# Two of the five feed-forwards: three matmuls of 288, 256 and 272 columns in place of three of 272, with the first 16 tokens' share added by VectorE

## The chip, the core and the metric

One core of one Trainium2 chip runs the whole program: TensorE (PE, with its weight loads shown apart as PEld), VectorE (DVE), ScalarE (ACT), GpSimd (POOL) and SyncE (SP, which issues the loads of the weights). The metric is the device time of one execution in microseconds; the median of the runs shown counts.

## What is computed

The reference runs two blocks after one another on one sequence of 256 tokens, 1024 wide. The first block puts 16 learned tokens (`meta`) ahead of the sequence and drops them at its end, so its layers work on 272 tokens, except the last feed-forward, of which only 256 tokens are needed.

```
h = concat(meta, x)                                    # 16 + 256 tokens
for l in range(2):
    h = h + 0.5 * swiglu(rmsnorm(h), ffn1_gate, ffn1_up, ffn1_down)
    h = h + hybrid_mixer(rmsnorm(h), ...)
    h = h + 0.5 * swiglu(rmsnorm(h), ffn2_gate, ffn2_up, ffn2_down)
x = rmsnorm(h)[:, 16:]
# then second_block(x): ffn, attention, ffn, ffn, retention, ffn, on 256 tokens
swiglu(x) = (silu(x @ w_gate) * (x @ w_up)) @ w_down   # 1024 -> 2816 -> 1024
```

## The kernel before

The program is a list of phases (`PHASES`), numbered y: 0 feed-forward, 1 mixer, 2 feed-forward, 3 feed-forward, 4 mixer, 5 feed-forward, and so on. Tokens lie along the columns, so a phase with all tokens has matmuls of 272 columns (y = 0 to 4) and the later ones 256 (`first_col`, `width`). The change is about y = 2 and y = 3.

Each float32 operand is split in two parts, a high one and the rest, the low one: the weights into `whi` and `wlo` (ACT copies `raw` to `whi`, L435, and DVE subtracts, L442), the input into `u` (ACT L467, DVE L480) and the hidden values into `hid` (ACT L1187, DVE L1669). A product of one 128 by 128 weight tile then takes three matmuls that add up in one PSUM bank, here called a triple: high weights with the high input (L419), high weights with the low input (L426), low weights with the high input (L427). `products` writes them, and each brings its own weight load.

A feed-forward streams its weights in panels through a ring of four (`RING`). A gate or up panel has 8 weight tiles, a down panel 11. The 44 gate and up panels come first (`gate_up`): for each pair, called a tile here, DVE multiplies both results by the norm's factor `R` (`gt` L1658, `up` L1660), ACT takes the Silu (`sl` L1182), DVE multiplies (`pr` L1665), and both split the product into `hid`. Between these DVE and ACT split the panels four ahead. Then 16 down panels give 8 tiles of the output (`out_proj`), which DVE adds to `h` (L1625); ACT and DVE split the new `h` at once into the next phase's `u`, and POOL sums its squares (L521, L524) for the next norm, which PE averages with a matmul (L562) behind the next phase's first panel. A feed-forward has 44 × 8 + 16 × 11 = 528 triples.

The order on each engine is the order in which the code is written; semaphores tie the engines together. PE waits for a split panel (`lo_ready`), for an emptied bank (`a_evac`: the one used four panels before) and, in a phase's first panel, for `u_ready`: for six of the eight tiles of `u` at its first weight tile, and for the last two at weight tiles 6 and 7. `U_PLACE` and `HID_PLACE` say at how many columns past the start of the buffer the high part stands, and by how many more the low part is shifted; tiles lie 320 columns apart in phases 0 to 4.

## Time and profile before

| | |
|---|---|
| median of 3 runs | 2170.9 us (2170.79 to 2171.69) |
| the profiled execution's own time | 2170.45 us |
| its span, first to last instruction | 2168.7 us |
| PE busy | 2157.2 us, 99% of the span, 18129 matmuls |
| DVE, ACT, POOL busy | 1471.9, 1205.7, 283.8 us |
| matmuls of 272 columns in `u` and `hid` | 1504 and 528 of each line of the triple |

Busy time of PE counts a matmul from its start to the end of its last column, and neighbours overlap, so a row's mean of 281 ns is no pace. The pace of a run of matmuls is read from their start times: the time from one start to the next, or a stretch divided by the number of starts in it. The profiled execution is 0.45 us below the median and lies 1.75 us above its own span.

### The profile page before, as it was taken

What the parts mean: (1) busy time and instruction counts of PE and PEld (TensorE: products, weight loads), DVE (VectorE), ACT (ScalarE), POOL (GpSimd) and SP (SyncE); (2) the same over time, 40 slices, a digit from 0 to 9 for tenths busy, and PEclk for the clock granted to TensorE, in tenths of its full rate; (3) what the DMA queues carried; (4) which work ended last, traced back from release to release, by engine and by line L of the source; (5) the groups of instructions that cost most, each with busy time, mean ns of one, the idle gap of its engine ahead of it and who ended that gap; (6) DMA issues with size and microseconds to landing.
All of it is one profiled execution on the core that took longest, in us unless ns stands there. A gap on an engine that the chain in (4) does not pass through costs nothing.

```text
span 2168.7 us, 48303 instructions
## 1 busy us (share of the span) xinstructions
PE 2157.2 (99%) x18129; PEld 2139.8 (99%) x18129; DVE 1471.9 (68%) x2242; ACT 1205.7 (56%) x1757; POOL 283.8 (13%) x328
## 2 busy tenths in 40 slices
PE   8999999999999999999999999999999999999999
PEld 8999999999999999999999999999999999999999
DVE  6655998665566579876657657976656745686663
ACT  6444786544444368855545547865455535465552
POOL 0001661100100136220020011010010010101000
PEclk9999999999999999999999999999999999999999
DMA  6555435555455554456656655356656655446563
GB/s 233 176 192 167 163 117 175 175 174 198 153 179 187 182 164 142 150 179 193 204 176 195 204 190 170 119 183 194 207 173 196 210 177 181 159 156 196 193 219 129
DMA packets 100401, 386.57 MB, mean 178 GB/s; under 512 B 11312, under 2 KB 12464, under 8 KB 100304
## 3 DMA queue, kind: packets, MB, share of 16 engines
q1 hardware_dynamic: 99648, 383.89, 54.0%
q0 software_dynamic: 368, 1.26, 0.2%
q8 instruction: 62, 1.02, 0.2%
q14 instruction: 35, 0.29, 0.0%
q10 hardware_dynamic: 288, 0.12, 0.0%
HBM read 384.18 MB, written 1.05 MB: 178 GB/s over the span
## 4 chain that ended last, share of the span: by engine, by line
PE 91%; DVE 6%; ACT 2%; issue 1%; DMA 0%; ACTq 0%; DVEq 0%
PE bank L426 28%; PE bank L427 28%; PE bank L419 28%; DVE wlo L442 2%; DVE bank L1723 1%; PE bank L1064 1%; PE bank L1066 1%; PE bank L1065 1%; ACT whi L435 1%; PE bank L1111 0%; PE bank L773 0%; DVE proj L1709 0%; PE bank L955 0%; PE bank L957 0%; PE bank L958 0%
## 5 line engine op out<-in xcount | busy, mean ns | idle before, releaser
L419 PE MATMUL bank<-u,whi 128*128 128x256 f32 (+2 forms) x3776 | 1062.6, 281 | 7.1 <-DVE u L480 7.1
L426 PE MATMUL bank<-u,whi 128*128 128x256 f32 (+1 forms) x3776 | 1062.0, 281 | 0.0
L427 PE MATMUL bank<-u,wlo 128*128 128x256 f32 (+1 forms) x3776 | 1060.0, 281 | 0.0
L442 DVE TENSOR_TENSOR wlo<-raw,whi 128x1024 fp32r<-128x1024 f32 (+1 forms) x677 | 891.7, 1319 | 187.2 <-ACT whi L435 186.6
L435 ACT ACTIVATE whi<-raw 128x1024 fp32r<-128x1024 f32 (+1 forms) x677 | 743.5, 1112 | 189.6 <-PE bank L427 168.8
L419 PEld LDWEIGHTS bank<-u,whi 128*128 128x128 f32 x3776 | 711.2, 188 | 8.5 <-DVE wlo L442 7.1
L426 PEld LDWEIGHTS bank<-u,whi 128*128 128x128 f32 x3776 | 711.1, 188 | 0.9 <-issue 0.2
L427 PEld LDWEIGHTS bank<-u,wlo 128*128 128x128 f32 x3776 | 710.9, 188 | 0.0
L419 PE MATMUL bank<-hid,whi 128*128 128x256 f32 (+1 forms) x1408 | 394.2, 280 | 0.0
L426 PE MATMUL bank<-hid,whi 128*128 128x256 f32 (+1 forms) x1408 | 394.2, 280 | 0.0
L427 PE MATMUL bank<-hid,wlo 128*128 128x256 f32 (+1 forms) x1408 | 394.2, 280 | 0.0
L1660 DVE TENSOR_TENSOR up<-bank,R 128x256 f32<-128x256 f32 (+1 forms) x176 | 75.7, 430 | 289.9 <-PE bank L427 289.9
L427 PEld LDWEIGHTS bank<-hid,wlo 128*128 128x128 f32 x1408 | 264.6, 188 | 0.0
L426 PEld LDWEIGHTS bank<-hid,whi 128*128 128x128 f32 x1408 | 264.6, 188 | 0.0
L419 PEld LDWEIGHTS bank<-hid,whi 128*128 128x128 f32 x1408 | 264.6, 188 | 0.0
L467 ACT ACTIVATE u<-h,gain 128x256 fp32r<-128x256 f32 (+1 forms) x88 | 44.2, 512 | 268.4 <-DVE h L1625 262.5
L1182 ACT ACTIVATE sl<-gt 128x256 f32<-128x256 f32 (+1 forms) x160 | 67.7, 423 | 197.8 <-DVE gt L1658 197.7
L1187 ACT ACTIVATE hid<-pr 128x256 f32 (+2 forms) x160 | 67.9, 424 | 152.8 <-DVE pr L1665 152.8
L1625 DVE SCALAR_TENSOR_TENSOR h<-bank,h 128x256 f32<-128x256 f32 (+1 forms) x88 | 37.8, 430 | 164.0 <-PE bank L427 163.9
L516 POOL TENSOR_TENSOR ssq<-h 128x256 f32<-128x256 f32 (+1 forms) x10 | 6.2, 624 | 1028.7 <-DVE h L1625 1028.7
L2170 POOL TENSOR_TENSOR proj<-proj,tprod 128x272 f32<-128x272 f32 (+1 forms) x120 | 121.4, 1032 | 54.9 <-ACT tprod L1225 50.0
L521 POOL TENSOR_TENSOR sq<-h 128x256 f32<-128x256 f32 (+1 forms) x70 | 45.1, 645 | 345.7 <-DVE h L1625 344.7
(298 smaller groups left out, 2187.7 us busy)
## 6 DMA issues: line engine op xcount, KB each, us to landing
raw<-w SPq DMA_DIRECT2D x552, 512.0 KB, 3.4
raw<-w SPq DMA_DIRECT2D x128, 704.0 KB, 4.7
h<-xT SPq DMA_DIRECT2D x4, 272.0 KB, 5.8
outT<-h SPq DMA_DIRECT2D x8, 128.0 KB, 4.7
consts<-cst POOLq DMA_DIRECT2D x1, 576.0 KB, 4.5
dist<-cst POOLq DMA_DIRECT2D x1, 192.0 KB, 2.8
rdist<-cst POOLq DMA_DIRECT2D x1, 192.0 KB, 4.1
sgain<-small POOLq DMA_DIRECT2D x1, 145.5 KB, 5.1
```

The lines of the kernel that those rows point to most:

```text
L419: pe.matmul(out[:, cut:cols], w, x[:, cut:cols], start=first, stop=False, skip_group_check=True)
L426: pe.matmul(out, w_h, x_lo, start=False, stop=False, skip_group_check=True)
L427: return pe.matmul(out, w_l, x_hi, start=False, stop=last, skip_group_check=True)
L435: act.activation(weights(0, n), raw[:, n % RING, 0:COLS[n]].rearrange("p (k c) -> p k c", c=128), ACT.Copy).then_inc(hi_ready, 1)
L442: dve.tensor_tensor(weights(1, n), raw[:, n % RING, 0:COLS[n]].rearrange("p (k c) -> p k c", c=128), weights(0, n), ALU.subtract).then_inc ...
L467: act.activation(u_at(y, 0, f), h[:, f, win(y)], ACT.Copy, scale=norm_gain(y, f)).then_inc(u_hi_ready, 1)
L521: pool.tensor_tensor(sq[:, win(y)], h[:, f, win(y)], h[:, f, win(y)], ALU.mult).then_inc(sq_done, 1)
L1182: act.activation(sl[:, p, W], gt[:, p, W], ACT.Silu).then_inc(silu_done, 1)
L1187: act.activation(hid_at(y, 0, f), pr[:, p, W], ACT.Copy).then_inc(hid_hi_ready, 1)
L1625: dve.scalar_tensor_tensor(out=h[:, f, W], in0=src, scalar=factor, in1=h[:, f, W], op0=ALU.mult, op1=ALU.add).then_inc(h_done, 1)
L1660: dve.tensor_tensor(up[:, p, W], bank[(g + 1) % 4][:, 0:N], R[:, W], ALU.mult).then_inc(a_evac, 1)
L2170: pool.tensor_tensor(acc, acc, tprod[:, m % TAP_RING, W2], ALU.add)\
```

## The change

In phases 2 and 3 (`JOINED`) the triple is made by `joined_products`. The low part of the first 16 tokens' input is no longer beside the other low values but in the 16 columns just ahead of the high part. One matmul with the high weights takes these 16 columns and the 272 high ones as one run of 288 columns; another takes the other 256 low columns; the low weights still meet 272 columns. The columns are 816 before and after. The bank then holds 16 columns more: the first tokens' low product in columns 0 to 15, and everything else in 16 to 287. DVE adds these 16 columns where it empties the bank, in an instruction of its own, and writes the low parts in two pieces. Phase 2 issues the 288 columns first, phase 3 the 256.

```diff
-U_PLACE = {0: (48, 0), 1: (48, 0), 2: (48, 0), 3: (48, 0), 4: (48, 0), 5: (48, 0), 6: (48, 0), 8: (48, 0), 9: (48, 0), 10: (48, 0), 11: (48, 0), 12: (48, 0), 7: (48, 0)}
+U_PLACE = {0: (48, 0), 1: (48, 0), 2: (48, -16), 3: (64, -32), 4: (48, 0), 5: (48, 0), 6: (48, 0), 8: (48, 0), 9: (48, 0), 10: (48, 0), 11: (48, 0), 12: (48, 0), 7: (48, 0)}
-HID_PLACE = {0: (24, 0), 2: (24, 0), 3: (24, 0), 5: (24, 0), 7: (24, 0), 9: (24, 0), 10: (24, 0), 12: (24, 0)}
+HID_PLACE = {0: (24, 0), 2: (24, -16), 3: (40, -32), 5: (24, 0), 7: (24, 0), 9: (24, 0), 10: (24, 0), 12: (24, 0)}
+JOINED = (2, 3)
+LONG_FIRST = {2: True, 3: False}
...
+        def joined_products(pe, out, n, k, x_hi, x_lo, first, last, long_first):
+            w_h, w_l = weights(0, n)[:, k, :], weights(1, n)[:, k, :]
+            long, short = (out[:, 0:META + T], with_ahead(x_hi)), (out[:, 2 * META:META + T], x_lo[:, META:T])
+            for i, (o, x) in enumerate((long, short) if long_first else (short, long)):
+                pe.matmul(o, w_h, x, start=(first and i == 0), stop=False, skip_group_check=True)
+            return pe.matmul(out[:, META:META + T], w_l, x_hi, start=False, stop=last, skip_group_check=True)
...
     def dve_update(dve, y, f):
+            if y in JOINED:
+                dve.scalar_tensor_tensor(out=ahead(u_at(y, 0, f)), in0=h[:, f, 0:META], scalar=norm_gain(y, f),
+                                         in1=u_at(y, 0, f, 0, META), op0=ALU.mult, op1=ALU.subtract)
+                dve.scalar_tensor_tensor(out=u_at(y, 1, f, META), in0=h[:, f, META:T], scalar=norm_gain(y, f),
+                                         in1=u_at(y, 0, f, META), op0=ALU.mult, op1=ALU.subtract).then_inc(u_ready, 1)
+                return
...
     def act_norm(act, y):
+            if y in JOINED:
+                act.activation(R_long[:, 0:META], NORM[:, 0:META], ACT.Ln, bias=rms_eps)
+                act.activation(R, NORM[:, 0:T], ACT.Ln, bias=rms_eps).then_inc(log_done, 1)
+                act.wait_ge(log_done, n)
+                act.activation(R_long[:, :], R_long[:, :], ACT.Exp, scale=-0.5).then_inc(R_ready, 1)
+                return
...
             def out_proj(y, n0, per_tile, factor, N, sources=None, done=None, split_ahead=0):
+                    if y in JOINED:
+                        src = bank[4 + f % 2]
+                        dve.scalar_tensor_tensor(out=h[:, f, 0:META], in0=src[:, 0:META], scalar=factor,
+                                                 in1=h[:, f, 0:META], op0=ALU.mult, op1=ALU.add).then_inc(first_added, 1)
+                        dve.scalar_tensor_tensor(out=h[:, f, META:T], in0=src[:, 2 * META:META + T], scalar=factor,
+                                                 in1=h[:, f, META:T], op0=ALU.mult, op1=ALU.add)
+                        dve.wait_ge(first_added, adds(y) + 2 * FT + f + 1)
+                        dve.scalar_tensor_tensor(out=h[:, f, 0:META], in0=src[:, META:2 * META], scalar=factor,
+                                                 in1=h[:, f, 0:META], op0=ALU.mult, op1=ALU.add).then_inc(h_done, 1)
...
                 def tile(n, g, F, f, p, it, last, split=True):
+                        if y in JOINED:
+                            dve.tensor_tensor(long[:, p, :], src[:, 0:META + T], R_long[:, :], ALU.mult).then_inc(a_evac, 1)
+                            dve.wait_ge(a_evac, g + i + 1 + it4)
+                            dve.tensor_tensor(out[:, p, 0:META], out[:, p, 0:META], long[:, p, 0:META], ALU.add)\
+                               .then_inc(first_added, 1)
...
+                    if y in JOINED:
+                        dve.tensor_tensor(ahead(hid_at(y, 0, f)), pr[:, p, 0:META], hid_at(y, 0, f)[:, 0:META], ALU.subtract)
+                        dve.tensor_tensor(hid_at(y, 1, f)[:, META:T], pr[:, p, META:T], hid_at(y, 0, f)[:, META:T],
+                                          ALU.subtract).then_inc(hid_ready, 1)
```

ACT's Silu and DVE's product wait for the adds (`first_added`) in place of `a_evac`. `R`, `gt` and `up` become parts of longer buffers `R_long`, `gt_long` and `up_long`, in all phases.

On PE the first two triples of phase 2 stand as follows before the change (rows name the operation, the bank it writes, the input and the weights it reads, and its output's size).

```order
L419 MATMUL bank<-u,whi 128x272
L426 MATMUL bank<-u,whi 128x272
L427 MATMUL bank<-u,wlo 128x272
L419 MATMUL bank<-u,whi 128x272
L426 MATMUL bank<-u,whi 128x272
L427 MATMUL bank<-u,wlo 128x272
```

After the change the same place reads so.

```order
L451 MATMUL bank<-u,whi 128x288
L451 MATMUL bank<-u,whi 128x256
L452 MATMUL bank<-u,wlo 128x272
L451 MATMUL bank<-u,whi 128x288
L451 MATMUL bank<-u,whi 128x256
L452 MATMUL bank<-u,wlo 128x272
```

Nothing moved from its place; only two of the three sizes are others. On DVE one tile of gate and up (the last but one of phase 2, where no loop counters stand between) is before the change:

```order
L1658 TENSOR_TENSOR gt<-bank,R 128x272
L1660 TENSOR_TENSOR up<-bank,R 128x272
L442 TENSOR_TENSOR wlo<-raw,whi 128x1408
L1665 TENSOR_TENSOR pr<-sl,up 128x272
L442 TENSOR_TENSOR wlo<-raw,whi 128x1408
L1669 TENSOR_TENSOR hid<-pr,hid 128x272
```

After it, the same tile:

```order
L1727 TENSOR_TENSOR gt_long<-bank,R_long 128x288
L1729 TENSOR_TENSOR gt_long<-gt_long 128x16
L1727 TENSOR_TENSOR up_long<-bank,R_long 128x288
L1729 TENSOR_TENSOR up_long<-up_long 128x16
L467 TENSOR_TENSOR wlo<-raw,whi 128x1408
L1740 TENSOR_TENSOR pr<-sl,up_long 128x272
L467 TENSOR_TENSOR wlo<-raw,whi 128x1408
L1745 TENSOR_TENSOR hid<-pr,hid 128x16
L1746 TENSOR_TENSOR hid<-pr,hid 128x256
```

Three instructions of 16 columns came in per tile, and both splits of panels stand behind two of them. On DVE the end of phase 2 (the last two tiles of `h`, the splits of phase 3's first panels and the last of its `u`) is before the change:

```order
L1625 SCALAR_TENSOR_TENSOR h<-bank,h 128x272
L442 TENSOR_TENSOR wlo<-raw,whi 128x1024
L480 SCALAR_TENSOR_TENSOR u<-h,gain,u 128x272
L442 TENSOR_TENSOR wlo<-raw,whi 128x1024
L1625 SCALAR_TENSOR_TENSOR h<-bank,h 128x272
L480 SCALAR_TENSOR_TENSOR u<-h,gain,u 128x272
L442 TENSOR_TENSOR wlo<-raw,whi 128x1024 x2
```

After it, from the last tile of `h` on:

```order
L1682 SCALAR_TENSOR_TENSOR h<-bank,h 128x16
L1684 SCALAR_TENSOR_TENSOR h<-bank,h 128x256
L1687 SCALAR_TENSOR_TENSOR h<-bank,h 128x16
L509 SCALAR_TENSOR_TENSOR u<-h,gain,u 128x16
L511 SCALAR_TENSOR_TENSOR u<-h,gain,u 128x256
L467 TENSOR_TENSOR wlo<-raw,whi 128x1024 x2
```

One instruction on `h` became three, and one on `u` became two; their order against the splits stays.

## Rows read from the trace of the kernel before

**Rows 1.** The page: busy time of each engine, TensorE's granted clock by slice.

```profile
PE 2157.2 (99%) x18129; PEld 2139.8 (99%) x18129; DVE 1471.9 (68%) x2242; ACT 1205.7 (56%) x1757; POOL 283.8 (13%) x328
PEclk9999999999999999999999999999999999999999
```

**Rows 2.** Timeline of PE: first matmul of phases 2, 3 and 4 (start, length).

```profile
384.98 0.29 PE L419 MATMUL bank<-u,whi 128*128 128x272 f32 x1
...
580.81 0.29 PE L419 MATMUL bank<-u,whi 128*128 128x272 f32 x1
...
776.63 0.29 PE L419 MATMUL bank<-u,whi 128*128 128x272 f32 x1
```

**Rows 3.** Busy time by stretch: phase 2 (272 columns) and 7 (256).

```profile
400.00:500.00 100.00, 100.00 (x813) 100.00 (x812) 63.34 (x103) 48.41 (x67) 0.00 (x0) 1.00 0.54 178
...
1220.00:1290.00 70.00, 70.00 (x620) 70.00 (x619) 42.98 (x57) 31.49 (x39) 4.75 (x8) 1.00 0.62 204
```

**Rows 4.** Timeline of PE: first and last of 43 matmuls of 512 columns.

```profile
1801.24 0.39 PE L1064 MATMUL bank<-whi,u 128*128 128x512 f32 x1
...
1810.86 0.39 PE L1064 MATMUL bank<-whi,u 128*128 128x512 f32 x1
```

**Rows 5.** Timeline of PEld: weight loads behind two matmuls of 288 columns, and the next.

```profile
259.63 0.19 PEld L419 LDWEIGHTS bank<-u,whi 128*128 128x128 f32 x1
...
259.76 0.19 PEld L426 LDWEIGHTS bank<-u,whi 128*128 128x128 f32 x1
...
879.19 0.19 PEld L419 LDWEIGHTS bank<-u,whi 128*128 128x128 f32 x1
...
879.33 0.19 PEld L426 LDWEIGHTS bank<-u,whi 128*128 128x128 f32 x1
```

**Rows 6.** Timeline of PE, phases 1 and 4: first and last of 10, 11, 10.

```profile
284.64 0.29 PE L427 MATMUL bank<-u,wlo 128*128 128x272 f32 x1
...
285.78 0.29 PE L427 MATMUL bank<-u,wlo 128*128 128x272 f32 x1
...
897.01 0.28 PE L427 MATMUL bank<-u,wlo 128*128 128x256 f32 x1
...
898.19 0.28 PE L419 MATMUL bank<-u,whi 128*128 128x256 f32 x1
...
903.90 0.28 PE L427 MATMUL bank<-u,wlo 128*128 128x256 f32 x1
...
904.92 0.28 PE L427 MATMUL bank<-u,wlo 128*128 128x256 f32 x1
```

**Rows 7.** Timeline of DVE in phase 2: one tile, and the idle time before.

```profile
450.77 0.44 DVE L1660 TENSOR_TENSOR up<-bank,R 128x272 f32<-128x272 f32 x1 [2.16 <-PE bank L427]
...
456.69 0.44 DVE L1660 TENSOR_TENSOR up<-bank,R 128x272 f32<-128x272 f32 x1 [2.15 <-PE bank L427]
```

**Rows 8.** DVE's instructions by form: busy, mean ns of one.

```profile
L1665 DVE TENSOR_TENSOR pr<-sl,up 128x256 f32<-128x256 f32 x110 | 46.0, 418 | 0.0
...
L1665 DVE TENSOR_TENSOR pr<-sl,up 128x272 f32<-128x272 f32 x66 | 28.7, 434 | 0.7 <-ACT sl L1182 0.7
...
L1931 DVE TENSOR_SCALAR dst<-dst,lam 128x2 f32<-128x2 f32 x8 | 1.8, 229 | 0.3
```

**Rows 9.** Timeline from phase 2 to 3, by engine.

```profile
581.01 0.44 DVE L1625 SCALAR_TENSOR_TENSOR h<-bank,h 128x272 f32<-128x272 f32 x1 [3.38 <-PE bank L427]
582.04 0.50 DVE L480 SCALAR_TENSOR_TENSOR u<-h,gain,u 128x272 fp32r<-128x272 f32 x1 [0.59 <-ACT u L467]
...
582.25 0.93 POOL L524 TENSOR_TENSOR ssq<-ssq,sq 128x272 f32<-128x272 f32 x1
...
583.40 0.28 PE L419 MATMUL bank<-u,whi 128*128 128x272 f32 x1
...
583.77 0.39 PE L562 MATMUL bank<-ssq,consts 128*128 128x272 f32 x1
```

More of the change, by code:

```diff
@@ L396, in hid_at, with ahead, with_ahead @@
             return tile_of(hid, FT, TILE_STEP if y <= LAST_MIX else SEQ, HID_PLACE[y], y, part, f, first_col(y), T)
+        def ahead(whole):
+            return bass.AP(whole.tensor, whole.offset - META, [whole.ap[0], [1, META]])
+        def with_ahead(whole):
+            return bass.AP(whole.tensor, whole.offset - META, [whole.ap[0], [1, META + T]])
         def width(y):
@@ L451, in da_square, with adds @@
             return dqk[:, f // 2, f % 2, :] if f < 4 else (dsq if f < 6 else drq)[:, f % 2, :]
+        def adds(y):
+            return (2 * FT + KD) * JOINED.index(y)
         def norm_gain(y, f):
@@ L683, in tile @@
                                 pe.wait_ge(ready, count - (lag if K == 0 else last - K))
+                            if y in JOINED:
+                                mm = joined_products(pe, bank[4 + j % 2], n, k, x(0, K), x(1, K),
+                                                     K == 0, K == last, LONG_FIRST[y])
+                                continue
                             mm = products(pe, bank[4 + j % 2][:, 0:N], n, k, x(0, K), x(1, K),
@@ L1198, in ffn @@
                     n = b["P"] + 2 * f
-                    act.wait_ge(a_evac, b["A"] + 2 * f + 1)
+                    if y in JOINED:
+                        act.wait_ge(first_added, adds(y) + 2 * f + 1)
+                    else:
+                        act.wait_ge(a_evac, b["A"] + 2 * f + 1)
                     act.activation(sl[:, p, W], gt[:, p, W], ACT.Silu).then_inc(silu_done, 1)
@@ L1624, in out_proj @@
                     dve.wait_ge(panel_used, n0 + (done[f] if done else per_tile * (f + 1)))
-                    dve.scalar_tensor_tensor(out=h[:, f, W], in0=src, scalar=factor,
-                                             in1=h[:, f, W], op0=ALU.mult, op1=ALU.add).then_inc(h_done, 1)
+                    if y in JOINED:
+                        src = bank[4 + f % 2]
[6 more added lines that the diff above has]
+                                                 in1=h[:, f, 0:META], op0=ALU.mult, op1=ALU.add).then_inc(h_done, 1)
+                    else:
+                        dve.scalar_tensor_tensor(out=h[:, f, W], in0=src, scalar=factor,
+                                                 in1=h[:, f, W], op0=ALU.mult, op1=ALU.add).then_inc(h_done, 1)
                     if per_tile == 1 and f > 0:
@@ L1656, in tile @@
                     it4, it2 = (RING * it, 2 * it) if not last else (0, 0)
-                    dve.wait_ge(panel_used, n + 1 + it4)
-                    dve.tensor_tensor(gt[:, p, W], bank[g % 4][:, 0:N], R[:, W], ALU.mult).then_inc(a_evac, 1)
-                    dve.wait_ge(panel_used, n + 2 + it4)
-                    dve.tensor_tensor(up[:, p, W], bank[(g + 1) % 4][:, 0:N], R[:, W], ALU.mult).then_inc(a_evac, 1)
+                    for i, (out, long) in enumerate(((gt, gt_long), (up, up_long))):
+                        src = bank[(g + i) % 4]
+                        dve.wait_ge(panel_used, n + i + 1 + it4)
+                        if y in JOINED:
+                            dve.tensor_tensor(long[:, p, :], src[:, 0:META + T], R_long[:, :], ALU.mult).then_inc(a_evac, 1)
+                            dve.wait_ge(a_evac, g + i + 1 + it4)
+                            dve.tensor_tensor(out[:, p, 0:META], out[:, p, 0:META], long[:, p, 0:META], ALU.add)\
+                               .then_inc(first_added, 1)
+                        else:
+                            dve.tensor_tensor(out[:, p, W], src[:, 0:N], R[:, W], ALU.mult).then_inc(a_evac, 1)
                     if split:
@@ L1663, in tile @@
                     dve.wait_ge(silu_done, F + 1 + it2)
-                    dve.wait_ge(a_evac, g + 2 + it4)
+                    if y in JOINED:
+                        dve.wait_ge(first_added, adds(y) + 2 * (f if last else p) + 2 + it4)
+                    else:
+                        dve.wait_ge(a_evac, g + 2 + it4)
                     dve.tensor_tensor(pr[:, p, W], sl[:, p, W], up[:, p, W], ALU.mult).then_inc(prod_done, 1)
```

23 lines of the change are left out of this document (17 added, 6 removed).

## The prediction

> **What bounds the kernel now.** I read the page first: PE is busy for 99% of the span, at the upper level of its granted clock (2.4 GHz) in every slice [rows 1]. So the question is what a triple costs, and whether anything makes PE wait. The timeline of PE at the ends of phases 2 and 3 gives the place of the change: phase 2 runs from 384.98 to 580.81 us, phase 3 from there to 776.63 us, 195.8 us each [rows 2]. The list of waits for that stretch is empty on PE: inside the two phases PE waits for nobody, and a faster engine elsewhere would be worth nothing. Only shorter matmuls help.
>
> The busy time by stretch gives their pace. In a stretch of 100 us of phase 2, 813 matmuls lie wholly or in part. A matmul is shown for about 0.29 us, so 2.3 of them are open at any moment, and 100 / (813 − 2.3) gives 123.3 ns from start to start. For 256 columns it is 70 / (620 − 2.4) = 113.3 ns [rows 3]. 512 columns take 42 starts in 9.62 us, 229.0 ns each [rows 4]. So 512 columns cost twice 256 and 1% more, while the 16 columns from 256 to 272 cost 10.0 ns, where a sixteenth of 113.3 would be 7.1. That is the odd size: 272 pays about 2.9 ns that 256 does not.
>
> **The change on PE.** A phase has 528 triples, two phases 1056. Before, a triple costs 3 × 123.3 = 370.0 ns. Now it has 288, 256 and 272 columns. Two sizes have rows: 113.3 and 123.3. For 288 there is no stream in the trace, so I bound it:
> - by the line from 256 to 512 columns, 113.3 + 32 × (229.0 − 113.3) / 256 = 127.8 ns, that is 9 times a 32nd column at a pace of 256's;
> - by the line from 272 to 512, 123.3 + 16 × (229.0 − 123.3) / 240 = 130.3 ns, if 288 carries 272's surcharge along;
> - by a second step of 10.0 ns, 133.3 ns.
>
> There are a few single matmuls of 288 columns (L730, in the mixers). The weight load behind one and the one after it lie 0.13 us apart in one place and 0.14 in another [rows 5], which bounds it by 125 and 145 and decides little, but does not point above the third. I take 127.8, since 256 and 512, both whole multiples of 32 columns, lie on one line and 288 is such a multiple too. The triple is then 127.8 + 113.3 + 123.3 = 364.4 ns, 5.6 ns less, and 1056 × 5.6 = 5.9 us less. By the second bound the triple is 366.9 and the gain 3.3 us; by the third it is 369.9 and the gain nothing.
>
> The Trainium skill speaks against this change: "TensorE: Matmul & The Clock Gate", section "Back-to-back issue gap", gives N / 2.4 + 2.5 ns for an isolated warm matmul of N columns. By it 272 columns would take 115.8 ns and the sum depends on the columns alone, 816 before and after, so that PE would gain nothing. This trace disagrees with both its size (123.3) and its slope (10.0 ns for 16 columns after 256).
>
> **VectorE.** Per tile of gate and up it gets three instructions of 16 columns and two that grow by 16. The growth is 434 − 418 = 16 ns each. The nearest small instruction, on 2 columns, takes 229 ns; the 16 columns by their slope alone would take 16 ns [rows 8]. I take 200 ns each, with the wait of each add for its own engine's result in it: 0.6 + 0.03 us per tile, between 0.1 and 0.9. The cover is DVE's idle time before it empties the up panel, 2.16 us in each tile's 5.92 us [rows 7]; behind the waiting instruction stand the split of the panel four ahead and ACT's Silu, which PE needs two panels later. About 1.5 us of cover remain, 1.3 in the worst case. So this costs nothing; without the cover it would be 44 × 0.63 = 28 us.
>
> **The two ends.** When a phase ends, the last tile of `h` is updated (581.01 us), ACT and DVE split it (DVE's part starts at 582.04 and ends at 582.54), and PE needs it at 583.40, weight tile 7 of the next first panel. POOL's last sum ends at 583.18, and PE's norm matmul starts at 583.77 [rows 9]. The update becomes three instructions, which adds about 0.38 us (0.05 to 0.46), and the split of `u` in two adds 0.2 more into phase 3. Then `u` is ready at 583.1 and the sum at 583.6: both in time, by 0.3 and 0.2 us. If the small instructions are slower than I think, PE stalls by some tenths twice; I put 0.1 us for both. ACT's extra logarithm of 16 columns delays the first emptied bank by less than 0.5 us, and PE comes back to that bank four panels, 11.8 us, after the phase's start. The 8 further small instructions on `u` at the end of phase 1 come one per panel of 24 matmuls, 3.0 us; with 0.2 us each I count nothing for them. No DMA is added; SP's loads wait for the splits as before.
>
> **The sum.** The profiled execution's 2170.45 us − 5.9 + 0.1 = 2164.65 us; the median of the runs is 0.45 above the profiled one, so 2165.1 us.
>
> **The rivals.**
> - *288 costs more than the line* (130 to 132 ns). For it: 272 does not lie on the line either, and where the place of the columns against the weights changes from triple to triple, as it now does within a triple (288 starts 16 columns ahead of the others in phase 2, 272 starts 16 behind in phase 3), some surcharge may come back. Gain 1.5 to 3.3 us: 2168 to 2169.5 us.
> - *Only the sum of the columns counts.* Then 288 costs a second 10.0 ns and the triple 369.9: 2171 us, and the change does nothing, which is also what the skill's formula says. Against it: 512 columns would have to cost 113.3 + 16 × 10.0 = 273 ns, and they cost 229.0.
> - *PE falls into its slower pace.* The trace shows that the same matmul has two paces at the same granted clock. In the mixers 272 columns ran at 1.14 / 9 = 126.7 ns for a whole panel, and 256 columns at 1.18 / 10 = 118.0 ns, while the same line 6 us later has 1.02 / 9 = 113.3 [rows 6]. Each pace holds until something interrupts the stream. In phases 2 and 3 all 272-column matmuls ran at the faster pace; the change shifts starts by 16 columns against the weights, and the norm matmul behind the first panel interrupts once per phase. Locked in the slower pace from there, a triple costs about 132 (127.8 and the 4.7 of the 256) + 118.0 + 126.7 = 377, 7 ns more than before, and both phases 7.4 us more: 2178 us. One phase of the two: near 2172. The change loses from 44% of the triples on (5.6 against 7.0).
> - *VectorE or the ends make PE wait.* 0.5 us at each end at most, or a tile's worth if the cover were gone; 2166 to 2172 us.
>
> **How the numbers follow.** The line (2164 to 2166.5 us) gets 0.43; the dearer 288, 0.24; columns alone, 0.14; the slower pace in one phase 0.06, in both 0.08; waits 0.05. Runs of this kernel agree within 0.04%, and about 0.2%, 4.3 us, is what a measurement can tell from no change. Faster by more than that is below 2166.6: the line and a little of the second and of the waits, 0.48. Slower is above 2175.2: 0.09. The rest, 0.43, is within. My range is 2162.5 to 2171.8: below, 272 may lose its surcharge too when its neighbours are whole multiples (2.9 ns × 1056 = 3.1 us, half of which I allow); above, it ends past the cases of columns alone and one slow phase. Left out are about 0.08 above and 0.05 below and at the edges of waits. The likeliest case's own range is 2164 to 2166.5.
>
> **What the changed profile would show.** Right: phases 2 and 3 last 192.8 us each in place of 195.8; in a stretch of 100 us of either, about 825 matmuls in place of 813; the 256 columns at 113.3 ns; DVE's idle time before `up` still above 1 us per tile; no wait of PE inside the phases. The step that fails first if I am wrong is the price of 288: from 133 ns on there is no gain. A pace of 118 for the 256 columns would show the slower pace, by phase, since the two phases differ in order and places; a gap on PE at either end longer than that around the norm matmul now would show the ends.

## The result and the profile after

The changed kernel takes 2179.1 us (median of 7 runs, 2178.01 to 2179.78), the kernel before 2171.1 us in the same comparison (7 runs, 2170.68 to 2172.55). The ratio is 1.0035 with a 95% interval of 1.0026 to 1.0044: slower by 8.0 us, where 2165.1 was forecast and the range ended at 2171.8. The profiled execution took 2179.65 us, its span is 2177.9.

The page, for [rows 1]: PE is still busy for 99%, at the upper level of its clock throughout. Its busy time grew by 8.0 us with the same number of matmuls. DVE has 180 instructions more.

```profile
PE 2165.2 (99%) x18129; PEld 2147.5 (99%) x18129; DVE 1504.1 (69%) x2422; ACT 1206.6 (55%) x1759; POOL 278.9 (13%) x328
...
PEclk9999999999999999999999999999999999999999
```

Busy time by stretch of the changed kernel, in the columns of [rows 3]: phase 2, phase 3, phase 7.

```profile
400.00:500.00 100.00, 100.00 (x813) 100.00 (x813) 72.27 (x153) 48.44 (x68) 0.00 (x0) 1.00 0.55 178
600.00:700.00 100.00, 100.00 (x792) 100.00 (x791) 69.78 (x149) 47.99 (x67) 0.00 (x0) 1.00 0.55 175
...
1220.00:1290.00 70.00, 70.00 (x620) 70.00 (x619) 43.13 (x61) 33.17 (x41) 3.33 (x5) 1.00 0.64 207
```

Phase 2 has the 813 starts that it had before, where 825 were forecast; by the prediction's own formula that is again 123.3 ns a matmul, 370.0 a triple. Phase 3 fell to 792, 100 / (792 − 2.3) = 126.6 ns, 380 a triple. Phase 7 is untouched.

The timeline of PE shows the sizes one by one (a row with x2 holds two matmuls of one line, its start is that of the first): phase 2, long one first, and phase 3, short one first.

```profile
451.15 0.28 PE L451 MATMUL bank<-u,whi 128*128 128x256 f32 x1
451.26 0.28 PE L452 MATMUL bank<-u,wlo 128*128 128x272 f32 x1
451.38 0.41 PE L451 MATMUL bank<-u,whi 128*128 128x288 f32 x2
451.63 0.29 PE L452 MATMUL bank<-u,wlo 128*128 128x272 f32 x1
...
782.79 0.29 PE L451 MATMUL bank<-hid,whi 128*128 128x288 f32 x1
782.92 0.29 PE L452 MATMUL bank<-hid,wlo 128*128 128x272 f32 x1
783.05 0.42 PE L451 MATMUL bank<-hid,whi 128*128 128x256 f32 x2
783.30 0.29 PE L452 MATMUL bank<-hid,wlo 128*128 128x272 f32 x1
```

The 256 columns start at 451.15, the 272 behind them at 451.26, the next 288 at 451.38, and one 272 to the next is 0.37 us. In phase 3 that is 0.38. The start times of a whole stretch, which the trace has in ns, give the means: in phase 2 288 columns take 133.0 ns, 256 take 114.5, 272 take 122.5, together 370.0; in phase 3 130.0, 123 and 127, together 380.

The list of waits from 383 to 800 us was empty on PE before. Now it has one row, and the timeline shows where: the start of phase 2, in its first panel.

```profile
PE bank L451 <- DVE u L511: 1.5, 3, 0.6
```
```profile
384.84 0.29 PE L444 MATMUL bank<-qk,wlo 128*128 128x272 f32 x1
385.74 0.49 PE L451 MATMUL bank<-u,whi 128*128 128x288 f32 x2 [0.61 <-DVE u L511]
...
387.91 0.28 PE L452 MATMUL bank<-u,wlo 128*128 128x272 f32 x1
388.70 0.52 PE L451 MATMUL bank<-u,whi 128*128 128x288 f32 x2 [0.51 <-DVE u L511]
389.06 0.28 PE L452 MATMUL bank<-u,wlo 128*128 128x272 f32 x1
389.76 0.52 PE L451 MATMUL bank<-u,whi 128*128 128x288 f32 x2 [0.42 <-DVE u L511]
...
390.24 0.39 PE L596 MATMUL bank<-ssq,consts 128*128 128x272 f32 x1
...
787.16 0.39 PE L596 MATMUL bank<-ssq,consts 128*128 128x272 f32 x1
```

PE's starts are 0.90, 0.79 and 0.70 us apart at the three gaps, and the first matmul behind each takes some 0.1 us longer. DVE's last `u` part had come too late, and the timeline of DVE says why. First the changed kernel, then the kernel before, each from one split of a weight panel to the next:

```profile
379.38 1.80 DVE L467 TENSOR_TENSOR wlo<-raw,whi 128x1024 fp32r<-128x1024 f32 x1
381.10 0.43 DVE L1690 SCALAR_TENSOR_TENSOR h<-bank,h 128x272 f32<-128x272 f32 x1
381.45 0.22 DVE L509 SCALAR_TENSOR_TENSOR u<-h,gain,u 128x16 fp32r<-128x16 f32 x1
381.59 0.93 DVE L511 SCALAR_TENSOR_TENSOR u<-h,gain,u 128x256 fp32r<-128x256 f32 x1
382.45 1.79 DVE L467 TENSOR_TENSOR wlo<-raw,whi 128x1024 fp32r<-128x1024 f32 x1
```
```profile
380.37 1.28 DVE L442 TENSOR_TENSOR wlo<-raw,whi 128x1024 fp32r<-128x1024 f32 x1 [0.30 <-ACT whi L435]
382.20 0.44 DVE L1625 SCALAR_TENSOR_TENSOR h<-bank,h 128x272 f32<-128x272 f32 x1 [0.55 <-PE bank L427]
382.55 0.49 DVE L480 SCALAR_TENSOR_TENSOR u<-h,gain,u 128x272 fp32r<-128x272 f32 x1
383.35 1.28 DVE L442 TENSOR_TENSOR wlo<-raw,whi 128x1024 fp32r<-128x1024 f32 x1 [0.30 <-ACT whi L435]
```

Before, DVE waited twice in the panel shown, of 2.98 us, 0.30 for ACT and 0.55 for PE: PE set the pace. Now there is no wait left in its 3.07 us; DVE is the slower one. The small instruction itself takes only 0.14 us from start to start. But the split went from 1.28 to 1.79 and the `u` part from 0.49 to 0.93, with fewer columns. POOL, which squares and adds `h` at the same time, went the other way: its square (L521 before, L555 now) took 0.83 us and takes 0.64, its sum (L524, L558) took 1.63 and takes 0.84. First the kernel before, then the changed one:

```profile
379.73 0.83 POOL L521 TENSOR_TENSOR sq<-h 128x272 f32<-128x272 f32 x1 [0.29 <-DVE h L1625]
380.64 1.63 POOL L524 TENSOR_TENSOR ssq<-ssq,sq 128x272 f32<-128x272 f32 x1
```
```profile
379.25 0.84 POOL L558 TENSOR_TENSOR ssq<-ssq,sq 128x272 f32<-128x272 f32 x1
381.60 0.64 POOL L555 TENSOR_TENSOR sq<-h 128x272 f32<-128x272 f32 x1 [1.51 <-DVE h L1690]
```

**Where the 9.2 us between the two spans lie**, by the starts of the norm matmuls: from that of phase 1 to that of phase 2 181.87 us in place of 179.49 (+2.4, the stall); to that of phase 3 195.89 in place of 195.82 (+0.1); to that of phase 4 201.03 in place of 195.83 (+5.2); the other 1.5 in code that the change does not touch, of which 1.3 in one stretch near the end, between the norm matmuls that start at 1791.87 and 1988.32 us before: 196.45 us, now 197.77.

DVE inside phase 2, for [rows 7] and [rows 8]: one tile from its first emptied bank on.

```profile
450.83 0.46 DVE L1727 TENSOR_TENSOR gt_long<-bank,R_long 128x288 f32<-128x288 f32 x1
451.33 0.17 DVE L1729 TENSOR_TENSOR gt_long<-gt_long 128x16 f32<-128x16 f32 x1
453.06 0.46 DVE L1727 TENSOR_TENSOR up_long<-bank,R_long 128x288 f32<-128x288 f32 x1 [1.56 <-PE bank L452]
```

The idle time before `up` went from 2.16 to 1.56 us: the 0.6 us of the forecast, and still hidden. The end of phase 2, for [rows 9]:

```profile
583.30 0.17 DVE L1682 SCALAR_TENSOR_TENSOR h<-bank,h 128x16 f32<-128x16 f32 x1 [3.11 <-PE bank L452]
583.39 0.41 DVE L1684 SCALAR_TENSOR_TENSOR h<-bank,h 128x256 f32<-128x256 f32 x1
...
584.63 0.48 DVE L511 SCALAR_TENSOR_TENSOR u<-h,gain,u 128x256 fp32r<-128x256 f32 x1
584.69 1.05 POOL L558 TENSOR_TENSOR ssq<-ssq,sq 128x272 f32<-128x272 f32 x1
586.13 0.62 PE L596 MATMUL bank<-ssq,consts 128*128 128x272 f32 x2
```

Phase 3 starts at 583.10, so that its eighth triple is due 7 × 0.38 us later, at 585.76; `u` is ready at 585.11, the sum at 585.74, the norm matmul runs at 586.13. No gap.

### The profile page after: what moved, and what is told of

Same layout as the page of the kernel before. It is cut to its first block, busy times and chain, and to the rows that moved or that the text cites. A ratio compares the mean times of both kernels' runs of the same rounds, so it can differ in the third digit from the quotient of the medians.

```text
span 2177.9 us, 48605 instructions
## 1 busy us (share of the span) xinstructions
PE 2165.2 (99%) x18129; PEld 2147.5 (99%) x18129; DVE 1504.1 (69%) x2422; ACT 1206.6 (55%) x1759; POOL 278.9 (13%) x328
## 4 chain that ended last, share of the span: by engine, by line
PE 90%; DVE 7%; ACT 2%; issue 1%; DMA 0%; ACTq 0%; DVEq 0%
PE bank L443 22%; PE bank L444 22%; PE bank L436 22%; PE bank L451 12%; PE bank L452 6%; DVE wlo L467 3%; DVE bank L1803 1%; ACT whi L460 1%; PE bank L1113 1%; PE bank L1115 1%; PE bank L1114 1%; PE bank L1160 0%; PE bank L822 0%; DVE proj L1789 0%; PE bank L1004 0%
## 5 line engine op out<-in xcount | busy, mean ns | idle before, releaser
L436 PE MATMUL bank<-u,whi 128*128 128x256 f32 (+1 forms) x3072 | 860.4, 280 | 7.1 <-DVE u L514 7.1
L443 PE MATMUL bank<-u,whi 128*128 128x256 f32 (+1 forms) x3072 | 860.4, 280 | 0.0
L444 PE MATMUL bank<-u,wlo 128*128 128x256 f32 (+1 forms) x3072 | 858.3, 279 | 0.0
L444 PEld LDWEIGHTS bank<-u,wlo 128*128 128x128 f32 x3072 | 578.5, 188 | 0.0
L436 PE MATMUL bank<-hid,whi 128*128 128x256 f32 (+1 forms) x1056 | 293.3, 278 | 0.0
L443 PE MATMUL bank<-hid,whi 128*128 128x256 f32 (+1 forms) x1056 | 293.3, 278 | 0.0
L444 PE MATMUL bank<-hid,wlo 128*128 128x256 f32 (+1 forms) x1056 | 293.3, 278 | 0.0
L451 PE MATMUL bank<-u,whi 128*128 128x288 f32 (+1 forms) x1408 | 264.9, 287 | 1.5 <-DVE u L511 1.5
L452 PE MATMUL bank<-u,wlo 128*128 128x272 f32 x704 | 202.9, 288 | 0.0
L443 PEld LDWEIGHTS bank<-hid,whi 128*128 128x128 f32 x1056 | 198.3, 188 | 0.0
L444 PEld LDWEIGHTS bank<-hid,wlo 128*128 128x128 f32 x1056 | 198.3, 188 | 0.0
L436 PEld LDWEIGHTS bank<-hid,whi 128*128 128x128 f32 x1056 | 198.3, 188 | 0.0
L1234 ACT ACTIVATE sl<-gt_long 128x256 f32<-128x256 f32 (+1 forms) x160 | 67.7, 423 | 212.1 <-DVE gt_long L1732 149.5
```

The source lines that it names most:

```text
L436: pe.matmul(out[:, cut:cols], w, x[:, cut:cols], start=first, stop=False, skip_group_check=True)
L443: pe.matmul(out, w_h, x_lo, start=False, stop=False, skip_group_check=True)
L444: return pe.matmul(out, w_l, x_hi, start=False, stop=last, skip_group_check=True)
L451: pe.matmul(o, w_h, x, start=(first and i == 0), stop=False, skip_group_check=True)
L452: return pe.matmul(out[:, META:META + T], w_l, x_hi, start=False, stop=last, skip_group_check=True)
L1234: act.activation(sl[:, p, W], gt[:, p, W], ACT.Silu).then_inc(silu_done, 1)
```

## The experiments

My theory after this profile was that 288 columns cost more than the line by themselves; the rivals were the start columns of the streamed operand, which now differ within a triple, the order, and the columns of the bank. The first four kernels ask for these one by one. Each ran once, beside a run of the kernel before at 2170.12 us on the same chip.

**Whole sizes.** All three matmuls of a triple read the long piece in phase 2, two of three in phase 3.

```diff
+            if long_first:
+                pe.matmul(long[0], w_h, long[1], start=first, ...)
+                pe.matmul(long[0], w_h, long[1], start=False, ...)
+                return pe.matmul(long[0], w_l, long[1], ...)
...
-            return pe.matmul(out[:, META:META + T], w_l, x_hi, ...)
+            return pe.matmul(long[0], w_l, long[1], ...)
```

> This kernel leaves out part of the sums: in phase 2 all three matmuls of a triple are 288 columns from the same place into the same columns (the low product of 256 tokens is left out and the high one taken twice); in phase 3 the triple is 256, 288 and 288. Theory 'starts': sizes that are whole multiples of 32 cost what the line says (127.8 and 113.3 ns) as long as neighbours start at the same place; the surcharge in the changed kernel comes from starts that move by 16 columns from one matmul to the next. Then phase 2 has 128 ns per matmul (about 784 matmuls in 100 us) and phase 3 keeps a surcharge, since 256 and 288 start at one place and the last at another only by the place of the first column. Theory 'size': 288 columns cost 130 to 133 ns in any company: phase 2 at 131 to 133 (755 to 766 in 100 us). Theory 'half step': only the 272 columns, no multiple of 32, upset their neighbours: phase 3 at (113.3 + 127.8 + 127.8) / 3 = 123.0 (816 in 100 us). In both theories with a surcharge phase 3 is at 127 or more (790 or fewer).

2193.72 us. The stretch of phase 2:

```profile
400.00:500.00 100.00, 100.00 (x753) 100.00 (x752) 67.12 (x142) 44.45 (x63) 0.00 (x0) 1.00 0.51 163
```

753 starts are 133.2 ns for each 288, all from one start column and to one bank column. In phase 3 it took 131 and 132, the 256 beside it 117. So 288 is dear without unequal neighbours too: the line's 127.8 was wrong for this stream.

**Shift alone.** The kernel before, three times 272, with the low parts 16 columns off against the high ones (in phase 2 the high ones were moved, in phase 3 the low ones).

```diff
-U_PLACE   2: (48, 0),  3: (48, 0)      HID_PLACE   2: (24, 0), 3: (24, 0)
+U_PLACE   2: (32, 16), 3: (48, -16)    HID_PLACE   2: (8, 16), 3: (24, -16)
```

> The kernel before with three matmuls of 272 columns; only the low inputs of phase 2 start 16 columns later, and those of phase 3 16 columns earlier, against the high ones (modulo 64 columns). Theory 'starts': the pace gets worse without any change in size, from 123.3 ns to 125 to 127 in at least one of the phases (790 to 802 matmuls in 100 us). Theories 'size' and 'half step': nothing changes, 123.3 ns (813).

2175.79 us.

```profile
400.00:500.00 100.00, 100.00 (x799) 100.00 (x798) 61.54 (x100) 47.65 (x67) 0.00 (x0) 1.00 0.55 178
600.00:700.00 100.00, 100.00 (x805) 100.00 (x805) 62.44 (x101) 48.48 (x67) 0.00 (x0) 1.00 0.55 176
```

Without any new size a matmul went from 123.3 to 125.5 ns in phase 2 and to 124.4 in phase 3 (by the start times); single ones lie between 120 and 130. So the starts seem to have a part too. It is one execution; against it stand nine phases of the old triple, in seven profiles of this case, all at 123.3.

**Orders swapped**, and **bank columns alike**.

```diff
-LONG_FIRST = {2: True, 3: False}
+LONG_FIRST = {2: False, 3: True}
```

> The changed kernel with the 256 columns first in phase 2 and the 288 first in phase 3, the places unchanged. If the order alone made phase 3 slow (126.6 ns per matmul against 123.3 in phase 2), the two phases trade paces: 792 matmuls in 100 us of phase 2, 813 of phase 3. If the places made it ('starts'), phase 3 stays near 792 and phase 2 near 813. Theory 'size' says neither moves.

2182.29 us. Phase 2 now has 792 starts in 100 us (256 at 117.0, 288 at 136.0, 272 at 127.0: 380.0), phase 3 has 799 (376.7). The 380 went with the order, but phase 3 did not get phase 2's 370 for it.

```diff
-            long, short = (...), (out[:, 2 * META:META + T], x_lo[:, META:T])
+            long, short = (...), (out[:, 0:SEQ], x_lo[:, META:T])
...
-            return pe.matmul(out[:, META:META + T], w_l, x_hi, ...)
+            return pe.matmul(out[:, 0:T], w_l, x_hi, ...)
```

> The changed kernel with all three outputs of a triple starting at the bank's column 0 in place of 0, 32 and 16 (the columns are then added up wrongly; only the time counts). If the place in PSUM makes the surcharge, both phases get faster, towards 121.5 ns (825 in 100 us). By the theories 'starts', 'size' and 'half step' nothing changes: 813 and 792.

2180.47 us, 813 and 792 starts as in the changed kernel. The bank's columns play no part.

The next four shared a run of the kernel before at 2171.25 us.

**Phase 2 alone.**

```diff
-U_PLACE   3: (64, -32)    HID_PLACE   3: (40, -32)
-JOINED = (2, 3)
+U_PLACE   3: (48, 0)     HID_PLACE   3: (24, 0)
+JOINED = (2,)
```

> Only phase 2 joined; phase 3 is that of the kernel before. Theory 'two causes' (a stall of some 2.3 us at the end of phase 1, and phase 3's pace of 126.6 ns): the stall stays, phase 2 has 813 matmuls in its stretch of 100 us, phase 3 has 813 too, and the time is 2.3 to 2.7 us over the kernel before. Rival 'a pace carried along' (phase 3 is slow because of what phase 2 left PE in): phase 3 stays near 792 to 800 and the time is 5 us or more over before.

2173.41 us, 2.2 over; the same three gaps at the end of phase 1, 813 starts in both phases. Phase 2's stream costs nothing and gains nothing; the stall is the whole loss.

**Phase 3 alone, made like phase 2.**

```diff
-JOINED = (2, 3)
-LONG_FIRST = {2: True, 3: False}
-U_PLACE   2: (48, -16), 3: (64, -32)    HID_PLACE   2: (24, -16), 3: (40, -32)
+JOINED = (3,)
+LONG_FIRST = {3: True}
+U_PLACE   2: (48, 0),   3: (48, -16)    HID_PLACE   2: (24, 0),   3: (24, -16)
```

> Only phase 3 joined, with phase 2's places and the long one first; phase 2 is that of the kernel before. Theory 'two causes': no stall at the end of phase 1, since the small instructions on u now stand at the end of phase 2; phase 3 runs at 370 ns a triple, 813 in 100 us; the time is that of the kernel before within 0.7 us. Rival 'any joined phase costs a stall ahead of it': 2 us over before, with gaps on PE at the end of phase 2. Rival 'phase 3 itself is slower': about 792 in 100 us and 5 us over before.

2176.02 us, 4.8 over. No gap on PE, as expected, but 799 starts in phase 3: triples of 368 and 385 ns in turn, 376.7 on average, where the same instructions at the same places took 368 and 372 in phase 2. My theory of two fixed causes fell here: one stream has two paces.

**Other places** (long one first in both phases).

```diff
-U_PLACE   2: (48, -16), 3: (64, -32)    HID_PLACE   2: (24, -16), 3: (40, -32)
+U_PLACE   2: (16, -16), 3: (16, 16)     HID_PLACE   2: (72, -16), 3: (72, 0)
```

> Both phases joined, the long one first, with other start columns: counted modulo 64 from a boundary of 256 bytes, 288 starts at 32 and 256 and 272 at 48 (phase 2, gate and up), 288 at 48 and both others at 0 (phase 2, down), 288 at 32, 256 at 16, 272 at 48 (phase 3, gate and up), 288 at 48, 256 at 16, 272 at 0 (phase 3, down). Theory 'size and place': 288 keeps 130 to 134 ns wherever it starts, 256 and 272 are at 113 to 123 and 122 to 128, and no stretch gets below 368 ns a triple (817 in 100 us). Rival 'place alone': 288 falls to 128 in at least one of the four places, and that stretch runs at 365 ns a triple or less (825 or more in 100 us). The stall at the end of phase 1 stays in both.

2178.59 us. The triples took 373.4 (gate and up) and 377.8 (down) in phase 2, 373.3 and 380.0 in phase 3; the 288 averaged 132.5 to 135.9. None is under 370, and one comes to 380 with the long one first.

**Eight small instructions** in the kernel before.

```diff
+            if y == 2:
+                hi = u_at(y, 0, f, 0, META)
+                dve.scalar_tensor_tensor(out=bass.AP(hi.tensor, hi.offset - META, [hi.ap[0], [1, META]]), in0=h[:, f, 0:META],
+                                         scalar=norm_gain(y, f), in1=hi, ...)
```

> The kernel before with one thing more: at the end of phase 1 eight DVE instructions of 16 columns on u, one ahead of each of the eight instructions that make u's low part for phase 2; nobody reads what they write, and the place is the gap ahead of u. Theory 'the extra instruction makes DVE the bound there': a panel costs DVE 3.0 to 3.1 us where PE wants 2.96, PE stalls near 385 to 389 us, and the time is 1 to 2.5 us over before. Rival 'it is the shifted start and the shorter form of the big instruction, or the split weights, not the extra one': no gap on PE there, within 0.4 us of before.

2173.47 us, 2.2 over. The list of waits on PE from 383 to 800 us, and DVE's timeline:

```profile
PE bank L419 <- DVE u L485: 1.6, 3, 0.7
```
```profile
379.74 1.79 DVE L442 TENSOR_TENSOR wlo<-raw,whi 128x1024 fp32r<-128x1024 f32 x1
381.46 0.43 DVE L1630 SCALAR_TENSOR_TENSOR h<-bank,h 128x272 f32<-128x272 f32 x1
381.81 0.22 DVE L482 SCALAR_TENSOR_TENSOR u<-h,gain,u 128x16 fp32r<-128x16 f32 x1
381.95 0.95 DVE L485 SCALAR_TENSOR_TENSOR u<-h,gain,u 128x272 fp32r<-128x272 f32 x1
```

The same three gaps and the same 1.79 and 0.95 us: the extra instruction is enough for the stall, without the shifted parts or the shorter form.

It does not always bring it, though. Of the twelve profiles with such an instruction at the end of phase 1 eleven have the stall; the run with whole sizes, which changes nothing there, has not. Its list of waits on PE from 383 to 800 us is empty, and from phase 1's norm matmul to phase 2's it took 179.81 us, 0.3 more than before. In its first panel, and in the four behind it, POOL had the long times:

```profile
369.59 0.48 DVE L515 SCALAR_TENSOR_TENSOR u<-h,gain,u 128x256 fp32r<-128x256 f32 x1
...
369.61 0.96 POOL L559 TENSOR_TENSOR sq<-h 128x272 f32<-128x272 f32 x1 [1.65 <-DVE h L1694]
370.65 1.63 POOL L562 TENSOR_TENSOR ssq<-ssq,sq 128x272 f32<-128x272 f32 x1
```

DVE gained time in these panels and met the long times only from 382.96 us on, too late to hold up PE. So the same instructions have two outcomes.

The next four, beside 2172.57 us, asked for the two paces and for what a size costs.

**Both phases like phase 2** (long one first, phase 2's places in phase 3).

```diff
-LONG_FIRST = {2: True, 3: False}
-U_PLACE   3: (64, -32)    HID_PLACE   3: (40, -32)
+LONG_FIRST = {2: True, 3: True}
+U_PLACE   3: (48, -16)    HID_PLACE   3: (24, -16)
```

> Both phases joined with phase 2's places and the long matmul first, so that phase 3 goes on in the stream that phase 2 ends in. Theory 'the pace is set where the stream begins, and carried' (the run with only phase 3 joined had the same instructions at 376.3 ns a triple that phase 2 runs at 370.0): phase 3 keeps phase 2's 370 ns, 813 matmuls in its stretch of 100 us, and the time is that of the run with phase 2 alone joined, 2.2 us over before. Rival 'the pace belongs to phase 3 itself, its weights or banks': about 799 in 100 us and 5.3 us over before. The stall at the end of phase 1 stays in both.

2176.28 us, and neither theory had it:

```profile
400.00:500.00 100.00, 100.00 (x799) 100.00 (x798) 71.68 (x151) 47.57 (x67) 0.00 (x0) 1.00 0.55 173
600.00:700.00 100.00, 100.00 (x813) 100.00 (x813) 72.42 (x152) 49.02 (x70) 0.00 (x0) 1.00 0.56 181
```

This time phase 2 is the slow one and phase 3 the fast. The starts tell when it changed: phase 2 ran at 369 and 371 ns up to its first gaps, and at 368 and 385 from the norm matmul (390.4 us) on; phase 3 kept 368 and 385 up to its norm matmul (589.7 us) and ran at 368 and 372 behind it. An interruption can change the pace, in either direction.

**A pause ahead of phase 3**: PE waits for all of `u`, in the kernel with phase 3 alone joined, and in the changed kernel.

```diff
-                                pe.wait_ge(u_ready, u_base(y) + (KD - 2 if k == 0 else k + 1))
+                                pe.wait_ge(u_ready, u_base(y) + (KD if y == 3 else KD - 2 if k == 0 else k + 1))
```

> The run with only phase 3 joined (phase 2's places, long first), and one thing more: PE waits at the start of phase 3 until all of u is there, a pause of about 2 us, after which the stream starts afresh. Theory 'the pace is set where the stream begins': phase 3 now runs at 370 ns a triple (813 in 100 us) behind the pause, and the time is before plus the pause, 2.0 to 2.6 us, less than without the pause. Rival 'the pace belongs to phase 3 itself': still about 799, and 6.8 to 7.4 us over before.

> The changed kernel with the same pause at the start of phase 3 (its own places, short one first). Theory 'the pace is set where the stream begins': behind the pause phase 3 leaves its 380 ns a triple for a pace nearer 370 (800 to 813 in 100 us), and the time is at or below that of the changed kernel in spite of the pause, 2176 to 2179 us. Rival 'the order and places of phase 3 set the 380': still 792 in 100 us, and about 2180.5 to 2181.5 us.

The first took 2172.19 us, 0.4 below the run beside it where 2.0 to 2.6 over had been expected, with 813 starts in phase 3 and a pause of 2.1 us. The second took 2181.03, with 792: the pause was simply added. The 370 and 376.7 belong to one stream and are exchanged; the 380 of the short-first order is a matter of its own.

**What a size costs.**

```diff
-            long, short = (...), (...)
-            for i, (o, x) in enumerate(...): ...
-            return pe.matmul(out[:, META:META + T], w_l, x_hi, ...)
+            o, x = out[:, 0:size], with_ahead(x_hi)[:, 0:size]
+            if first:
+                pe.matmul(out[:, 0:META + T], w_h, with_ahead(x_hi), ...)
+            else:
+                pe.matmul(o, w_h, x, ...)
+            pe.matmul(o, w_h, x, ...)
+            return pe.matmul(o, w_l, x, ...)
...
+                                                     k == 0, k == KD - 1, {2: 272, 3: 280}[y])
...
+                                                     K == 0, K == last, {2: 256, 3: 264}[y])
```

> What a size costs: every triple of the two phases has three matmuls of one size, all read from the long piece's start column (64 past a boundary, as the 288 in phase 2) and written from the bank's first column: 272 in gate and up of phase 2, 256 in its down panels, 280 in gate and up of phase 3, 264 in its down panels; the first matmul of each panel alone keeps 288. The low parts are not read, so some of the product is left out. Theory 'about 10 ns for each 16 columns above 256': 113.3 for 256, 118 for 264, 123 for 272, 128 for 280, beside the 133 for 288 already seen. Rival 'whole multiples of 32 are cheap, others dear': 256 at 113, and 264, 272 and 280 all near or above 123. Rival 'a step at 256': 264 already at 122 to 123, and 272, 280 rising by less than 5 ns for 8 columns.

2179.85 us. From the start times: 256 columns 119.0 ns, 264 121.4, 272 126.6, 280 128.9; with the 288 of the first run, 133.3 at the same start. No step and no cheap multiple of 32: 8 columns more cost 2.4, 5.2, 2.3 and 4.4 ns, 14.3 for all 32, 0.45 a column, which is also the slope of the line from 256 to 512 in the prediction (115.7 / 256). None of my three theories fitted. By this reading the slope was right, and what differs is the 256 at its foot: 119.0 here, 118.0 in the slower pace of [rows 6], 113.3 in the faster. But the 272 of this scan, 126.6, is at the slower pace as well (126.7 in [rows 6], 123.3 in the old triple), and 288 comes from another run, whose pace is not known. In the faster pace 113.3 and 123.3 lie 10.0 apart, and 133.3 would be the same step again. The scan does not settle which it is.

**Order alone** (the changed kernel with phase 2's places in phase 3, short one first there).

```diff
-U_PLACE   3: (64, -32)    HID_PLACE   3: (40, -32)
+U_PLACE   3: (48, -16)    HID_PLACE   3: (24, -16)
```

> The changed kernel with phase 2's places in phase 3 too, and only the order kept: the short matmul first in phase 3. Theory 'the order makes the 380': phase 3 stays at 123, 130 and 127 ns (380 a triple, 792 in 100 us), 5.2 us over phase 2, about 2178 to 2180 us. Rival 'the places of phase 3 make it': 370 to 376.5 a triple (799 to 813 in 100 us), 2173 to 2177 us.

2178.16 us; 791 starts in phase 3 (118, 136 and 126 to 127 ns, 380). At these places the order makes the 380.

**The paces over many executions**: the two kernels with phase 3 alone, with and without the pause, and that with both phases like phase 2, unchanged, 11 runs each beside 27 of the kernel before (median 2171.15 us, 2169.48 to 2172.69).

> The run with both phases joined alike, timed over five rounds. In its one execution the norm matmul behind the first panel changed phase 2 from 371 to 376.5 ns a triple and phase 3 from 376.5 to 370. Theory 'drawn anew in each execution': the times scatter in steps of 3.4 us, between 2173 (both fast) and 2180 (both slow). Rival 'fixed by the program': all within 2 us of 2176.3, the step of 1.3 us that a late phase shows among them.

> The run with only phase 3 joined, long one first, timed over five rounds beside the same with a pause. Theory 'fixed by the program': all at 2175 to 2177, 4 to 5 us over before. Rival 'drawn anew': some executions near 2171 to 2172.

> The same with the pause of about 2 us at the start of phase 3, over five rounds. Theory 'fixed by the program': all at 2172 to 2174, below the run without the pause in every round, and 1 to 2.5 us over before. Rival 'drawn anew': some executions near 2176 or above, and no clear order between the two.

The ratios go by all runs and are not quotients of the two medians.

| kernel | median us | runs | ratio to before (95%) |
|---|---|---|---|
| both like phase 2 | 2172.66 | nine at 2171.90 to 2173.27, two at 2176.10 and 2176.61 | 1.0011 (1.0002 to 1.0020) |
| phase 3 alone | 2174.43 | 2173.30 to 2176.11 | 1.0016 (1.0007 to 1.0025) |
| phase 3 alone, pause | 2175.91 | five at 2171.47 to 2174.27, six at 2175.91 to 2177.53 | 1.0017 (1.0008 to 1.0026) |

The profiled execution of the kernel with the pause, at 2177.30 us this time, phase 3:

```profile
600.00:700.00 100.00, 100.00 (x799) 100.00 (x798) 69.75 (x148) 48.23 (x67) 0.00 (x0) 1.00 0.52 174
```

The same kernel had 813 in phase 3 at 2172.19 us. So the pace behind an interruption is not fixed by the program: "drawn anew" holds for the kernel with the pause, and for that with both phases, whose one profile had 799 and 813 and whose other has 813 in both. That the pause helps fell with it: its first execution was a lucky one. Without the pause phase 3 seems to have been slow in every execution: its two profiles have 799, and its times, less the 3.5 us of the slower pace (528 × 6.7 ns), fall on the range of before. That is read from times, not shown run by run.

## Why the prediction was wrong

From 2165.1 to 2179.1 are 14.0 us: 5.9 that were not gained, 5.2 lost in phase 3, 2.4 of stall; the 0.5 left over is within the scatter of the runs. The first term alone would have left the time at 2171, inside the range; the other two, for which the sum had nothing, took it out.

- **The price of 288 is the step that failed first**: "I take 127.8, since 256 and 512, both whole multiples of 32 columns, lie on one line and 288 is such a multiple too." It took 133.0 in phase 2, 130.0 in phase 3, and 130 to 136 on average in the other runs; the 128 appeared in turns only, each paid back by the next triple (368, then 385). The third bound, "a second step of 10.0 ns, 133.3 ns" and a triple of 369.9, is what phase 2 did (370.0), so the rival "columns alone" described it, though I argued against it with 512. The reason stays open. By the scan the slope of my line holds, 0.45 ns a column, and I had taken its foot, 113.3, from a faster pace than the one that 288 kept. But the scan ran at the slower pace, and a second step of 10.0 ns in the faster one, 113.3, 123.3, 133.3, is not excluded. (The aside "9 times a 32nd column at a pace of 256's" is no second source for 127.8: nine eighths of 113.3 are 127.5.)
- By the formula for an isolated matmul in the Trainium skill, "TensorE: Matmul & The Clock Gate", section "Back-to-back issue gap", the time of a triple goes by the sum of its columns alone. Phase 2 agrees with that (370.0 before and after, 816 columns each), phase 3 does not: 816 columns took 380. An estimate by the same formula for 288 columns, 122.5 ns, lies 10.5 below the 133.0 measured.
- **The order was not priced at all.** The prediction gave 256 ahead of 288 and 288 ahead of 256 one sum. Short first took 380 in each of five profiles, at both pairs of places tried; long first took 370 or 376.7 at phase 2's places and 376.7 at phase 3's (at the other places 373 to 380). The two kernels that differ in phase 3's order alone took 2178.16 us (one run) and 2172.66 (median of 11), 5.5 us apart. Why PE is slower in that order stays open: the bank's columns changed nothing, and the places changed only how the 380 divide (123, 130, 127 or 118, 136, 126).
- **The rival "slower pace"** named the right kind of thing, two paces at one clock that hold until something interrupts the stream, and 2178 us. But it meant another event: both phases at 377. Phase 2 stayed at 370, and the time came from an order and a stall; that 2178 is near 2179.1 is luck. I also took the faster pace of the two phases as given, since all their 272-column matmuls had run at it; for the new stream it is drawn.
- **"I count nothing for them"**, the 8 small instructions at the end of phase 1, cost 2.4 us; added alone to the kernel before they cost 2.2. I held their 0.2 us against a panel's 3.0 us of PE, and not against DVE's idle time in that panel, 0.85 us in two waits. Its own 0.14 us would have fitted into that. What I did not see is that DVE's other instructions there run side by side with POOL's, and that one more instruction can move the long times from POOL to DVE: 0.5 us in the split and 0.4 in the `u` part of each panel. It did so in eleven of twelve profiles.
- **DVE inside the phases, the ends, ACT, the queues**: as forecast. 0.17 us for a small instruction in place of 0.20, 1.56 us of idle time left where 1.5 were expected, no gap at the end of phase 2 or 3.

Of the signs named in advance, 192.8 us a phase, 825 starts and 113.3 for 256 failed; DVE's idle time over 1 us held, and no wait of PE inside the phases held but for the three gaps in phase 2's first panel. No version of the joined triple was clearly faster than the kernel before: its best triple equals the old one at 370.0, and where phase 2 is joined a stall of 2.2 to 2.4 us comes on top in all profiles but one.

## What to carry to other kernels

Splitting the same columns into unequal matmuls saves nothing unless a stream of the new sizes, in the new order, has been seen at a lower sum: price the sequence, not its parts, and let the slope and the foot of a line come from one pace. Where an instruction is added, hold it against the idle time of its own engine in that very panel, and look which engine works beside it. Where a stream has two paces, one execution of a kernel can mislead by 3 to 4 us here: a pause that seemed to save 4 us saved nothing over 11 runs.

## What was not expected of the hardware

- One stream of matmuls, the same instructions at the same places and the same granted clock, runs at 370.0 or 376.7 ns a triple, changes at an interruption (the norm matmul, a wait), and does so differently in two executions of one kernel. Unchanged code shows the like: the stretch near the end that took 196.45 us before and 197.77 after takes 196.2 to 196.5 us in some profiles and 197.8 in others, of one kernel too (196.18 and 197.76 with the pause).
- With the low operand 16 columns off against the high one, and no change of size, a matmul took 1.1 to 2.2 ns more. This is one execution, and a pace drawn slower in it is not excluded.
- DVE and POOL side by side at the end of phase 1 trade time: in one panel before, the split and `u` part took 1.28 + 0.49 us on DVE, POOL's square and sum 0.83 + 1.63; with one instruction more it is 1.79 + 0.93 and 0.64 + 0.83. The sums are 4.23 and 4.19 us. For the split and the sum, the one that starts later is the longer one: before, the split starts at 380.37 and POOL's sum behind it at 380.64; now POOL's sum starts at 379.25 and the split behind it at 379.38.
- The Trainium skill has a rule for this, in "SBUF — State Buffer", section "SBUF: two separate sides": a DVE instruction with two SBUF inputs and a GpSimd instruction that reads SBUF lock one pair of ports, and the one that starts first keeps it for its whole instruction. The rows of the split and the sum agree: the later of the two is longer by 0.5 us (DVE) or 0.8 (POOL), the earlier is not. Those of the `u` part and the square do not settle it: in the changed kernel `u` starts 0.01 us ahead of the square (381.59 and 381.60) and is the longer one, 0.93 for 0.49; with whole sizes it starts 0.02 us ahead (369.59 and 369.61), and the square is the longer one, 0.96 for 0.64. That the ports are what stretches them is not shown; no run took POOL away.
